# Second attention's projections taken by other columns, and its first scores issued ahead of the last projection unit

## The reference

```python
def gqa_attention(h, w_qkv, q_g, k_g, w_o, cos, sin):
    qkv = h @ w_qkv                                  # 1024 -> 1024 + 256 + 256
    q, k, v = jnp.split(qkv, [Q_WIDTH, Q_WIDTH + KV_WIDTH], axis=-1)
    q = apply_rope(rmsnorm(q.reshape(B, T, N_HEADS, HEAD_DIM), q_g), cos, sin)
    k = apply_rope(rmsnorm(k.reshape(B, T, N_KV_HEADS, HEAD_DIM), k_g), cos, sin)
    v = v.reshape(B, T, N_KV_HEADS, HEAD_DIM)
    # for each head: softmax(q k^T / 8) v, four query heads to one key/value head
    return o @ w_o
```

## Time and profile before

| | before |
|---|---|
| median of 3 runs | 2832.05 us (2831.9 to 2832.52) |
| the profiled execution | 2831.32 us |
| its span | 2829.4 us |
| PE busy | 2793.9 us, 99% of the span |
| PE weight loads busy | 2294.1 us, 81% |
| DVE, ACT, POOL busy | 1335.0, 1092.3, 1147.8 us (47, 39, 41%) |
| mean granted TensorE clock | 0.996 of full speed |
| the twelve units and the builds | about 1453 to 1526 us of the span |
| the attention of the second block | about 1526 to 1637 us |

### The profile page before, as it was taken

The page is one execution under the profiler, slowest core; times in us unless marked ns, Lnnn a source line. Parts: engine busy times, 40 slices in busy tenths (PEclk is TensorE's granted clock), DMA queues, the critical chain, the costliest instruction groups (busy, mean ns, idle before and its releaser), DMA issues.

```text
span 2829.4 us, 37674 instructions
## 1 busy us (share of the span) xinstructions
PE 2793.9 (99%) x13762; PEld 2294.1 (81%) x13762; DVE 1335.0 (47%) x1512; ACT 1092.3 (39%) x1588; POOL 1147.8 (41%) x472
## 2 busy tenths in 40 slices
PE   9999999999999999999989999999999999999999
PEld 8788788888878778888877788888888888888887
DVE  4167468863436548875267751123322642421232
ACT  3443334343342544333344643234343223432332
POOL 4433435444435024444434024444344434444443
PEclk9999999999999999999999999999999999999999
DMA  5322238742333016763321023323343323233332
GB/s 159 90 75 68 82 97 273 239 140 87 101 87 97 4 53 213 246 192 103 95 77 53 2 68 104 97 100 98 92 129 94 90 82 104 90 90 96 104 97 74
DMA packets 319811, 299.94 MB, mean 106 GB/s; under 512 B 16268, under 2 KB 251224, under 8 KB 319576
## 3 DMA queue, kind: packets, MB, share of 16 engines
q1 hardware_dynamic: 304680, 236.70, 28.2%
q10 hardware_dynamic: 15024, 61.75, 6.4%
HBM read 296.30 MB, written 2.11 MB: 105 GB/s over the span
## 4 chain that ended last, share of the span: by engine, by line
PE 46%; issue 36%; POOL 16%; DVE 1%; POOLq 0%; ACT 0%; DVEq 0%; ACTq 0%
POOL wlo L554 16%; PE ps L1991 8%; PE ps L1993 8%; PE ps L1992 8%; PE ps L1849 6%; PE ps L1851 6%; PE ps L1850 6%; PE ps L2262 1%; PE ps L2231 1%; PE ps L2205 1%; PE ps L2337 1%; PE ps L2015 0%; PE ps L2017 0%; PE ps L2016 0%; PE ps L1854 0%
## 5 line engine op out<-in xcount | busy, mean ns | idle before, releaser
L554 POOL TENSOR_TENSOR wlo<-raw,whi 128x1024 fp32r<-128x1024 f32 x444 | 1122.6, 2532 | 1642.4 <-ACT whi L612 1642.2
L1849 PE MATMUL ps<-xhi,whi 128*128 128x512 f32 x1824 | 718.9, 394 | 0.3
L1851 PE MATMUL ps<-xhi,wlo 128*128 128x512 f32 x1824 | 711.2, 390 | 0.0
L1850 PE MATMUL ps<-xlo,whi 128*128 128x512 f32 x1824 | 710.9, 390 | 0.0
L612 ACT ACTIVATE whi<-raw 128x1024 fp32r<-128x1024 f32 x444 | 466.6, 1053 | 285.8 <-PE ps L1993 168.4
L1991 PE MATMUL ps<-whi,ahi 128*128 128x512 f32 x1184 | 463.5, 391 | 7.8 <-issue 7.2
L1993 PE MATMUL ps<-whi,alo 128*128 128x512 f32 x1184 | 462.4, 391 | 0.0
L1992 PE MATMUL ps<-wlo,ahi 128*128 128x512 f32 x1184 | 462.3, 390 | 0.0
L1849 PEld LDWEIGHTS ps<-xhi,whi 128*128 128x128 f32 x1824 | 342.8, 188 | 72.8 <-issue 3.2
L1851 PEld LDWEIGHTS ps<-xhi,wlo 128*128 128x128 f32 x1824 | 342.6, 188 | 71.8
L1850 PEld LDWEIGHTS ps<-xlo,whi 128*128 128x128 f32 x1824 | 343.0, 188 | 70.3 <-issue 1.4
(11 more groups left out here) (274 smaller groups left out, 2911.5 us busy)
## 6 DMA issues: line engine op xcount, KB each, us to landing
adaraw<-in_ada_w ACTq DMA_DIRECT2D x64, 768.0 KB, 6.1
raw<-in_ffn_w_up SPq DMA_DIRECT2D x88, 512.0 KB, 4.0
raw<-in_mlp_w_in SPq DMA_DIRECT2D x64, 512.0 KB, 4.1
raw<-in_mlp_w_out SPq DMA_DIRECT2D x64, 512.0 KB, 3.7
raw<-in_gmlp_w_in SPq DMA_DIRECT2D x48, 512.0 KB, 3.8
raw<-in_sc_ssm_w_in SPq DMA_DIRECT2D x44, 512.0 KB, 3.8
raw<-in_ffn_w_down SPq DMA_DIRECT2D x44, 512.0 KB, 3.7
raw<-in_fox_w_in SPq DMA_DIRECT2D x24, 512.0 KB, 3.8
```

Source lines behind the costliest of these rows:

```text
L554: pool.tensor_tensor(wlo[:, j], raw[:, j], whi[:, j].bitcast(F32), ALU.subtract).then_inc(w_lo, 1)
L1849: pe.matmul(out, lh, rh, start=start, stop=False)
L1850: pe.matmul(out, lh, rl, start=False, stop=False)
L1851: return pe.matmul(out, ll, rh, start=False, stop=stop)
```

## The change

The thirds are cut otherwise. The first now takes q of heads 0 to 3 with k, the second q of heads 4 to 7 with v, and the third is as it was. A unit of the first two thirds is loaded by two DMAs of 128 x 2 x 256 instead of one of 128 x 2 x 512; so the semaphore counts that ACT waits for are no longer linear in the unit's number, and the loop of ACT in the layer before (`dn1`) is written out flat.

The first chain is then wide (512 columns: 4 heads of q and 4 of k) and has six DVE steps in a tile, the second is narrow (256 columns of q) and has five. `v2` is copied from the second third. On PE, two K builds, both Q builds and the scores of g = 0 move ahead of the last unit; the other two K builds stand between those scores and that unit. ACT copies `q1raw` after the exponentials of g = 0 instead of before them.

```diff
+    def loads_until(u):
+        return u // RING + 1 + min(max((u - U0["qkv"]) // RING + 1, 0), 2)
...
+    def sp_qkv_mixed(sp, h):
+        w = w_qkv.rearrange("p c (b m) -> p c b m", m=HALF)
+        for e in range(4):
+            u = U0["qkv"] + 4 * h + e
+            for k in range(2):
+                sp_load(sp, u, 0, 0, w[:, 2 * e + k, 0::2, 256 * h:256 * h + 256],
+                        t_dst(u % RING)[:, k].rearrange("p (b m) -> p b m", b=2))
...
@@ act_qkv
-        for e in range(13):
-            if e < 12:
-                act_whi(act, S + AHEAD, e, e % 4)
+        for e in range(12):
+            act_whi(act, S + AHEAD, e, e % 4)
             if e in (4, 8):
                 hh = e // 4 - 1
-                b0, nh = (4, 4) if hh == 0 else (0, 8)
+                b0, nh = (4, 8) if hh == 0 else (0, 4)
                 act.wait_ge(unit_done, S + e)
...
-                if hh == 0:
+                if hh:
                     for t in range(NT):
                         act.activation(v2[:, t], ps[:, b0 + t, 256:512], ACT.Copy).then_inc(v_ev, 1)
                 act.wait_ge(q_sum, 5 * hh + 4)
...
         for j in range(K_BUILDS):
-            act.wait_ge(bd_tp, j + 1)
+            act.wait_ge(bd_tp, j + 1 if j < 2 else j + 3)
             act.activation(kT[:, j], ps[:, j], ACT.Copy).then_inc(bd_ev_a, 1)
+
+    def act_q1_raw(act):      # called by ACT's attention at g == 1
         act.wait_ge(unit_done, END["qkv"])
...
@@ dve_qkv
         for hh in range(2):
-            b0, nh = (4, 4) if hh == 0 else (0, 8)
+            b0, nz = (4, 2) if hh == 0 else (0, 1)
+            nh = 4 * nz
...
-                if hh:
-                    step(dve.tensor_tensor(qr[:, t, 0:8], v3(ra), v3(rb), ALU.add))
-                else:
-                    twice = lambda x: v3(x).unsqueeze(2).to_broadcast([P, 4, 2, HD])
+                step(dve.tensor_tensor(qr[:, t, 4 * hh:4 * hh + 4], v3(ra[:, 0:256]), v3(rb[:, 0:256]), ALU.add))
+                if hh == 0:
+                    twice = lambda x: v3(x[:, 256:512]).unsqueeze(2).to_broadcast([P, 4, 2, HD])
                     step(dve.tensor_tensor(kr[:, t], twice(ra), twice(rb), ALU.add))
...
@@ pe_qkv
         units(1, range(4))
-        pe.wait_ge(q_step, 5 * 3 + 1)
+        pe.wait_ge(q_step, 6 * 3 + 1)
+        units(2, [0, 1])
+        pe.wait_ge(q_step, 24 + 5 * 3 + 1)
         pe.wait_ge(v_ev, 4)
-        units(2, range(3))
-        pe.wait_ge(q_step, 20 + 5 * 3 + 1)
-        for h in range(4):
-            for t in range(NT):
-                ins = pe.transpose(ps[:, h, t * P:(t + 1) * P], kr[:, t, h].rearrange("p b d -> p (b d)"), ident)
-            ins.then_inc(bd_tp, 1)
+        for j in range(2):
+            pe_build_k(pe, j)
+        for p in range(Q_FIRST):
+            pe_build_q(pe, p, 2 + p)
+        units(2, [2])
+        scores_gqa(pe, 0).then_inc(at_s, 1)
+        pe.wait_ge(bd_ev_d, Q_FIRST)
+        for j in range(2, 4):
+            pe_build_k(pe, j)
         units(2, [3])
-        pe.wait_ge(q_step, 40)
-        for p in range(Q_FIRST):
-            if p == 0:
-                pe.wait_ge(bd_ev_a, K_BUILDS)
-            pe_build_q(pe, p, 2 + p)
```

More of the change, by code:

```diff
@@ L409, in run, with run_flat @@
             body(q * RING + j, j)
+    def run_flat(eng, n, body):
+        for e in range(n):
+            body(e, e % RING)
+    def loads_until(u):
+        return u // RING + 1 + min(max((u - U0["qkv"]) // RING + 1, 0), 2)
     def wait_raw(eng, start, e, j):
@@ L413, in wait_raw @@
         if isinstance(e, int):
-            eng.wait_ge(raw_in[s], 16 * ((start + e) // RING + 1))
+            eng.wait_ge(raw_in[s], 16 * loads_until(start + e))
         else:
-            eng.wait_ge(raw_in[s], (e - j) * 4 + 16 * ((start + j) // RING + 1))
+            eng.wait_ge(raw_in[s], (e - j) * 4 + 16 * loads_until(start + j))
     def sp_value(sp, x):
@@ L491, in sp_pairs, with sp_t @@
             body(i)
-    def sp_t(sp, name, w, pairs, cols):
+    def sp_qkv_mixed(sp, h):
[5 more added lines that the diff above has]
+                        t_dst(u % RING)[:, k].rearrange("p (b m) -> p b m", b=2))
+    def sp_t(sp, name, w, pairs, cols, off=0):
         for h, c0 in enumerate(cols):
-            start = U0[name] + h * pairs
+            start = U0[name] + h * pairs + off
             run(sp, pairs, lambda e, j: sp_load(sp, start, e, j, t_src(sp, w, e, c0), t_dst((start + j) % RING)))
@@ L524, in _ @@
         sp_gate_rows(sp, 1)
-        sp_t(sp, "qkv", w_qkv, 4, [D, 0, HALF])
+        for h in range(2):
+            sp_qkv_mixed(sp, h)
+        sp_t(sp, "qkv", w_qkv, 4, [HALF], off=8)
         sp_t(sp, "o", w_o, 4, [0, HALF])
@@ L808, in act_jit @@
         if n:
-            run(act, n, lambda e, j: step(H + 3, 3, e, j))
+            (run_flat if name == "dn1" else run)(act, n, lambda e, j: step(H + 3, 3, e, j))
         if last:
@@ L1153, in beside @@
         def beside(g):
+            if g == 1:
+                act_q1_raw(act)
             if g == 4:
@@ L1657, in dve_qkv, with step @@
         dve.wait_ge(q_tab, 6)
+        def step(ins):
+            nonlocal n
+            ins.then_inc(q_step, 1)
+            n += 1
         for hh in range(2):
-            b0, nh = (4, 4) if hh == 0 else (0, 8)
+            b0, nz = (4, 2) if hh == 0 else (0, 1)
+            nh = 4 * nz
             w = nh * HD
@@ L1667, in dve_qkv @@
             dve.wait_ge(q_sum, 5 * hh + 5)
-            z = 1 - hh
             for t in range(NT):
[L1670 to L1678, removed]
+                v3 = lambda x: x.rearrange("p (h d) -> p h d", d=HD)
@@ L1680, in dve_qkv @@
+                v4 = lambda x: x[:, 0:w].rearrange("p (z h d) -> p z h d", z=nz, d=HD)
+                pair = lambda x, e: x[:, 0:w].rearrange("p (z h d e) -> p z h d e", z=nz, e=2, d=HD // 2)[:, :, :, :, e]
+                tabs = gcs[:, 0:nz, t, 1].rearrange("p z (d e) -> p z d e", e=2)
                 if n:
                     dve.wait_ge(q_step, n)
-                step(dve.tensor_tensor(v3(qn), src, hsum[:, 2, t, 0:nh].unsqueeze(2).to_broadcast([P, nh, HD]), ALU.mult))
+                step(dve.tensor_tensor(v3(qn[:, 0:w]), v3(ps[:, b0 + t, 0:w]),
+                                       hsum[:, 2, t, 0:nh].unsqueeze(2).to_broadcast([P, nh, HD]), ALU.mult))
@@ L1683, in dve_qkv @@
                 dve.wait_ge(q_step, n)
-                step(dve.tensor_tensor(v3(ra), v3(qn), gcs[:, z, t, 0].unsqueeze(1).to_broadcast([P, nh, HD]), ALU.mult))
+                step(dve.tensor_tensor(v4(ra), v4(qn), gcs[:, 0:nz, t, 0].unsqueeze(2).to_broadcast([P, nz, 4, HD]), ALU.mult))
                 for e in range(2):
-                    step(dve.tensor_tensor(pair(rb)[:, :, :, e], pair(qn)[:, :, :, 1 - e],
-                                           tabs[:, :, e].unsqueeze(1).to_broadcast([P, nh, HD // 2]), ALU.mult))
+                    step(dve.tensor_tensor(pair(rb, e), pair(qn, 1 - e),
+                                           tabs[:, :, :, e].unsqueeze(2).to_broadcast([P, nz, 4, HD // 2]), ALU.mult))
@@ L1693, in dve_qkv @@
                     step(dve.tensor_tensor(kr[:, t], twice(ra), twice(rb), ALU.add))
[L1694 removed]
+        assert n == 44
         for p in range(Q_FIRST):
[L1696 removed]
+            dve.wait_ge(bd_tp, 2 + p + 1)
             dve.tensor_scalar(qT[:, p], ps[:, 2 + p], HD ** -0.5, None, ALU.mult).then_inc(bd_ev_d, 1)
@@ L2188, in pe_cum, with pe_attn @@
         ins.then_inc(cum_mm, 1)
-    def pe_attn(pe, A, ptb, causal, scores, v_of, build=None):
+    def pe_attn(pe, A, ptb, causal, scores, v_of, build=None, begun=0):
         B, G = 64 * A, 32 * A
@@ L2219, in pe_attn @@
         for g in range(32 + LAG + 1):
-            if g < 32:
+            if begun <= g < 32:
                 if g >= 2:
@@ L2224, in pe_attn @@
             w = g - LAG
+            if w == 0 and A:
+                pe.wait_ge(q1_copied, 4)
             if 0 <= w < 32:
@@ L2251, in scores_gqa @@
         p, i = divmod(g, 4)
+        if g == 0:
+            pe.wait_ge(bd_ev_d, 1)
+            pe.wait_ge(bd_ev_a, 2)
         if g == 1:
[L2253 to L2256, removed]
+            pe.wait_ge(bd_ev_a, K_BUILDS)
+        if i == 0 and p:
             pe.wait_ge(bd_ev_d, min(p + 1, Q_FIRST))
@@ L2282, in pe_qkv, with pe_build_k @@
         units(1, range(4))
-        pe.wait_ge(q_step, 5 * 3 + 1)
+        pe.wait_ge(q_step, 6 * 3 + 1)
+        units(2, [0, 1])
+        pe.wait_ge(q_step, 24 + 5 * 3 + 1)
         pe.wait_ge(v_ev, 4)
-        units(2, range(3))
-        pe.wait_ge(q_step, 20 + 5 * 3 + 1)
-        for h in range(4):
-            for t in range(NT):
-                ins = pe.transpose(ps[:, h, t * P:(t + 1) * P], kr[:, t, h].rearrange("p b d -> p (b d)"), ident)
-            ins.then_inc(bd_tp, 1)
-        units(2, [3])
-        pe.wait_ge(q_step, 40)
-        for p in range(Q_FIRST):
-            if p == 0:
-                pe.wait_ge(bd_ev_a, K_BUILDS)
-            pe_build_q(pe, p, 2 + p)
```

(11 more changed lines are left out.)

## The result

| | before | after |
|---|---|---|
| median | 2832.31 us (2831.33 to 2833.03, 9 runs) | 2839.78 us (2836.31 to 2840.52, 9 runs) |
| ratio, 95% interval | | 1.0025 [1.0016, 1.0034] |
| the profiled execution | 2831.32 us | 2836.31 us |
| its span | 2829.4 us | 2834.4 us |
| PE busy | 2793.9 us | 2793.4 us |

The change is slower by 0.25%, in the direction and nearly by the amount forecast (2839.2). One thing has to be kept in mind: the profiled execution is the fastest of the nine. It is 5.0 us slower than the profiled one of before, while the medians are 7.5 apart. A second profile of the change (change_again) shows where the rest is.

What follows compares the result with a forecast made beforehand. PE bounds the kernel, busy 2793.9 of 2829.4 us, with at most 5.5 us to give back. Losses 0.35 + 5.8 + 2.2 + 2.3 + 0.9 = 11.6 us against 4.4 gained: 7.2 slower, 2839.2 us, range 2834.5 to 2842.5.

Steps and rivals of the forecast that it cites:

- The second chain: Before the K builds: the narrow chain starts late and meets two POOL splits, so PE waits 5.8 us for `qn`.
- The first chain: In the projections: the wide chain's four tiles fall in step with POOL's splits, 5.4 us each; PE waits 0.35 us.
- The clock behind the wait: At the builds and eleventh unit, after the 5.8 us wait: half speed for some 4.4 us, costing 2.2 us.
- The first scores: Before the scores of g = 0: ACT's `kT` copies stand behind its last split; PE loses 2.3 us.
- The second fall: Behind the 2.3 us idle before the first scores: the clock can fall again, half of 1.7, 0.9 us.
- The gains: Wait before the K builds, 1.5 us, and attention's start, 2.9 us: together 4.4 us given back.
- The loads and the flat loop: Sixteen half DMAs instead of eight, and ACT's written-out loop: cost nothing, with some 15 us of cover.
- The rival that the splits don't collide: DVE slips between POOL's splits, only the `kT` wait remains: 2.1 us faster, 2829.9 us; chance 10%.
- the one that the clock stays: The wait before the K builds comes but the clock stays up: 4.1 us slower, 2836.1 us; chance 22%.
- the two clock terms: Clock falls behind the wait before the K builds, 2.2 us, and behind that before the first scores, 0.9 us.
- the waits for DVE: PE's waits for DVE's two chains in the projections: 0.35 us for the first, 5.8 us for the second.

Runs made afterwards that it cites:

- change_again: The changed kernel itself, unedited, run once more for a second profile; 2840.44 us (ratio to before 1.0031), its profiled execution 2840.33 us.
- late_wo_splits: The changed kernel, with ACT's splits for the first three units of `w_o` waiting until DVE is through both chains; 2832.16 us (1.0001 to before).
- qn_ahead: The changed kernel, with the second chain doing its four `qn` first and PE waiting for those alone; 2832.24 us (1.0000 to before).
- fill: The changed kernel, with 44 resultless transposes on PE while it waits for the second chain's fourth `qn`; 2836.48 us (1.0014 to before).
- kt_first: The changed kernel, with ACT copying the first two K builds to `kT` before its last split; 2836.22 us (1.0015 to before).
- qn_ahead_kt_first: The changed kernel with both edits: second chain's four `qn` first, and first two `kT` copies before ACT's last split; 2827.36 us (0.9985 to before).

## Why the prediction was right, term by term

- **The second chain.** Forecast: `qn` 5.8 us late for PE. Measured: 5.62 us from 1509.38 to 1515.00 less the pace of 0.23, 5.4. Of this the two splits in the second chain are 4.0 (late_wo_splits) and the late start 1.2. The order in which DVE does its steps is what makes both count (qn_ahead).
- **The first chain.** Forecast: tiles in step with the splits, 5.4 us each, PE waits 0.35. Measured: `qn` to `qn` 5.26 to 5.37 us, four steps of over 2 us, the last `qn` at 1497.81, and PE's loss about 0.1. The chain came out 0.4 us shorter than forecast, and that is about what PE's wait for the second one fell short by.
- **The clock behind the wait.** Forecast 2.2 us, measured 2.4 and 2.9 in the two profiles (9.40 and 9.87 us from the first K build to the eleventh unit's last matmul, against 7.01 with the wait removed), and 2.3 by filling it. The prediction went by the row, in which 18 transposes brought the clock back, and fill bears it out: 44 transposes in a row held it at 1.00. The Trainium skill ("TensorE: Matmul & The Clock Gate", Part 4: PE-mode transpose) says that the full clock does not engage in transpose mode; the measurements here say otherwise.
- **The first scores.** Forecast 2.3 us. From 1524.40 to 1527.06 are 2.66, less 0.23: 2.4. The cause is the one named, ACT's last split (kt_first).
- **The second fall.** Forecast 0.9 as the mean of falling and not. It falls in the second profile of the change and in three variants that keep the wait (fill, late_wo_splits, qn_ahead), and not in the first profile: 1.6 us where it comes. The mean should have been nearer to 1.6; this term was too small by up to 0.7.
- **The gains.** Forecast 4.4 us. Measured as a whole, 4.4 (qn_ahead_kt_first). At the attention's start 0.23 + 0.62 us of waiting remain, where 1.1 were forecast. Part of the agreement may be luck: 1.7 of what was to be gained is the fall behind the exponentials, which the profile of before has and two others with an equal wait lack, so it is not shown that a usual run of before has it.
- **The loads and the flat loop.** Forecast nothing, and PE waits for no load in the projections. The working was looser than the result: four units less the landing are 18 us of cover (4 x 5.44 - 3.8), not some 15, and the "about 2 us to spare" of the first load inside the projections rest on no row shown.
- **The rival that the splits don't collide** is out by six long steps of DVE, and the one that the clock stays by both profiles.

The mechanism was right in its main steps: both new waits, their causes, and a fall of the clock behind each. That the median came out within 0.6 us is partly luck, since errors of opposite sign cancelled: the two clock terms were too small by 0.9 to 1.4 us together, the waits for DVE too large by 0.6. And the difference of the medians is not all made here. The second profile took 9.0 us more than that of before (2840.33 against 2831.32), of which 1.1 stand ahead of the projections: PE comes out of its longest wait at 1442.23 instead of 1441.13. So the change's own place cost some 7.9 us where 7.2 were forecast, by this pair of profiles; the first profile, with one fall, gives 5.9 (5.0, and 0.9 by which it was ahead at that point). What stays open is why the clock falls behind one wait of 1.94 us and not behind another of the same length, and which of the falls in the first block's attention a usual run of the kernel before has.

## What to carry to other kernels

When a consumer is moved ahead by one unit, ask what its producer does last, not how much it does: here a DVE chain of the same length cost 5.4 us or nothing, according to whether the four steps that free the banks stood among the others or ahead of them. Follow each new wait of the busiest engine to the queue of the engine that ends it; the copies that PE needed stood behind a split for weights of `w_o`, whose first unit PE takes at 1642.13, 117 us behind that split. And where the clock falls behind a wait, add what that costs, which was here 45 to 70% of the wait again.

## What the runs showed of the hardware

- A DVE instruction with both inputs in SBUF that meets a POOL split of 2.4 us is prolonged until about 0.3 us (256 columns) or 0.55 us (512) behind the split's end: `qr` of 256 columns took 2.50 us instead of 0.43, and `qr` and `kr` of 512 took 2.77 and 2.89 instead of 0.69. One that reads PSUM is not: `qn` took its 0.42 us at 1490.03, in the middle of a split. When the tile's own length plus this loss is near the period of POOL's instructions (3.2 + 2.1 against 5.44 us), the two fall in step, and here every one of the four tiles paid.
- Transposes keep TensorE's clock up (44 in 4.96 us, granted clock 1.00 throughout), and bring it back (18 at 1446.24). At half clock eight transposes took 1.97 us instead of 1.09.
- Behind the same wait the clock falls in one execution and not in the next: behind 2.58 us of idle time in the first block's attention in four of ten profiles, behind 2.27 us for `kT` in four of five, behind 1.94 us for the exponentials in one of three; behind the 1.32 and 1.23 us for `qn` it did not. Each such fall was worth about 1.6 us. Two profiles of one kernel can differ by 4 us, most of it by this, more than most edits of this size, so a difference between two profiles is to be read only after their clocks.
